# Third head's queries moved between the first two heads' score and turn work, and a weight conversion moved ahead of a square, in a six-layer fp32 kernel

## What is computed

```python
def mla_mixer(xn, cos, sin, w_in, q_norm, w_q_up, kv_norm, w_kv_up, w_out):
    h = xn @ w_in
    q_lat, kv_lat, k_rope, z = jnp.split(h, [...], axis=-1)
    q = (rms_norm(q_lat, q_norm) @ w_q_up).reshape(B, S, N_HEADS, QK_NOPE_DIM + QK_ROPE_DIM)
    q_nope = q[..., :QK_NOPE_DIM]
    q_rope = apply_rope(q[..., QK_NOPE_DIM:], cos[:, :, None, :], sin[:, :, None, :])
    kv = (rms_norm(kv_lat, kv_norm) @ w_kv_up).reshape(B, S, N_HEADS, QK_NOPE_DIM + V_HEAD_DIM)
    k_nope, v = kv[..., :QK_NOPE_DIM], kv[..., QK_NOPE_DIM:]
    k_rope = apply_rope(k_rope, cos, sin)
    o = causal_block_attention(q_nope, q_rope, k_nope, k_rope, v)
    return (o.reshape(B, S, D_INNER) * jax.nn.silu(z)) @ w_out
```

## Time and profile before

| what | us |
|---|---|
| median of 3 runs | 2753.75 |
| lowest and highest of them | 2748.66, 2754.22 |
| the profiled execution | 2755.0 |
| its span, from the first to the last instruction | 2753.2 |

### The profile page before, as it was taken

How to read it: one execution, slowest core, us unless ns; L and a number is a source line. 1 busy time by engine, 2 the same in 40 slices (tenths; PEclk the granted TensorE clock), 3 DMA queues, 4 the chain that set the end, 5 groups by cost and what they waited for, 6 DMA issues and landing times.

```text
span 2753.2 us, 31973 instructions
## 1 busy us (share of the span) xinstructions
PE 2706.2 (98%) x12918; PEld 2265.5 (82%) x12918; DVE 1581.5 (57%) x2307; ACT 1156.2 (42%) x1834; POOL 628.5 (23%) x401
## 2 busy tenths in 40 slices
PE   8999999999999999999999999999999999999998
PEld 6888888888878888888888887878888888778886
DVE  6656555344465646565565787644445678734443
ACT  4323322222356636432235777422224767522223
POOL 1000111011136626300005542410113442411100
PEclk9999999999999999999999999999999999999999
DMA  4332323323222222222322211223233221233332
GB/s 153 100 100 92 103 93 100 100 92 100 91 69 64 65 76 65 91 94 98 100 92 94 77 55 46 84 85 98 94 100 102 70 70 32 77 92 94 98 100 69
DMA packets 69412, 238.78 MB, mean 87 GB/s; under 512 B 7696, under 2 KB 10256, under 8 KB 69264
## 3 DMA queue, kind: packets, MB, share of 16 engines
q1 hardware_dynamic: 69264, 236.73, 26.8%
HBM read 234.60 MB, written 2.10 MB: 86 GB/s over the span
## 4 chain that ended last, share of the span: by engine, by line
PE 93%; DVE 4%; POOL 1%; ACT 1%; issue 1%; DMA 0%; SPq 0%; POOLq 0%; DVEq 0%; ACTq 0%
PE ps L414 29%; PE ps L416 29%; PE ps L415 29%; PE ps L510 1%; POOL acc L2280 1%; PE ps L729 1%; PE ps L728 1%; PE ps L440 1%; DVE xl L1518 1%; POOL t L2465 1%; PE ps L714 0%; DVE x L1540 0%; PE ps L571 0%; PE ps L570 0%; DVE ptl L1514 0%
## 5 line engine op out<-in xcount | busy, mean ns | idle before, releaser
L895 ACT ACTIVATE wh<-raw 128x1024 fp32r<-128x1024 f32 (+2 forms) x453 | 465.1, 1028 | 755.9 <-PE ps L416 750.7
L414 PE MATMUL ps<-xh,wh 128*128 128x512 f32 x1920 | 754.2, 393 | 0.0
L416 PE MATMUL ps<-xh,wl 128*128 128x512 f32 x1920 | 747.5, 389 | 0.0
L415 PE MATMUL ps<-xl,wh 128*128 128x512 f32 x1920 | 747.3, 389 | 0.0
L1506 DVE TENSOR_TENSOR wl<-raw,wh 128x1024 fp32r<-128x1024 f32 (+1 forms) x339 | 447.1, 1319 | 155.3 <-ACT wh L895 155.2
L414 PE MATMUL ps<-yh,wh 128*128 128x512 f32 x1088 | 427.7, 393 | 10.6 <-DVE yl L1514 9.0
L415 PE MATMUL ps<-yl,wh 128*128 128x512 f32 x1088 | 424.9, 391 | 0.0
L416 PE MATMUL ps<-yh,wl 128*128 128x512 f32 x1088 | 424.9, 391 | 0.0
L414 PEld LDWEIGHTS ps<-xh,wh 128*128 128x128 f32 x1920 | 360.6, 188 | 77.1 <-issue 2.6
L415 PEld LDWEIGHTS ps<-xl,wh 128*128 128x128 f32 x1920 | 360.6, 188 | 76.5 <-issue 2.6
L416 PEld LDWEIGHTS ps<-xh,wl 128*128 128x128 f32 x1920 | 360.4, 188 | 74.8
(11 more groups left out here) (255 smaller groups left out, 3667.6 us busy)
## 6 DMA issues: line engine op xcount, KB each, us to landing
raw<-in_ff SPq DMA_DIRECT2D x120, 512.0 KB, 3.6
raw<-in_pool_in SPq DMA_DIRECT2D x64, 512.0 KB, 3.3
raw<-in_conv_in SPq DMA_DIRECT2D x64, 512.0 KB, 3.3
raw<-in_pool_out SPq DMA_DIRECT2D x32, 512.0 KB, 3.3
raw<-in_qk SPq DMA_DIRECT2D x32, 512.0 KB, 3.6
raw<-in_pool_grp SPq DMA_DIRECT2D x16, 512.0 KB, 3.3
raw<-in_conv_out SPq DMA_DIRECT2D x16, 512.0 KB, 3.3
raw<-in_mla_z SPq DMA_DIRECT2D x16, 512.0 KB, 3.6
```

The source lines that it names most:

```text
L414: pe.do.matmul(o, lh, rh_, start=start, stop=False)
L415: pe.do.matmul(o, lh, rl_, start=False, stop=False)
L416: return pe.do.matmul(o, ll, rh_, start=False, stop=stop)
L895: act.do.activation(h[:, 0:ncol], r[:, 0:ncol], ACT.Copy).then_inc(*mark("whi", ("whi", k)))
```

## The change

In the first place, the two query products of head 2 are taken out of their place behind `turn(0)`. `rope_up(2)` goes between `qn 1` and `scores(1)`, and `q_up` of head 2 between `scores(1)` and `turn(0)`. ACT's `swap` of `qr 2` goes ahead of `turned(0)`, and DVE's `turned_cos(2)` ahead of `turn_low(0)`. POOL's program is not edited. In the second place, ACT asks in the turn of each of the first three rows of the last projection for the weights three units ahead, where it asked for two; DVE does so between `add_out` and `x_low`. All later heads and rows keep their order.

```diff
@@ pe_program, mla_layer
                 q_up(("qn", 1), unit["qo", 0], (0, 128, 256))
+                rope_up(2)
                 for h in range(1, 15):
                     scores(h)
+                    if h == 1:
+                        q_up(("qn", 2), unit["qe", 2], (0, 256, 512))
                     turn(h - 1)
                     if h % 2:
-                        rope_up(h + 1)
-                        q_up(("qn", h + 1), unit["qe", h + 1], (0, 256, 512))
+                        if h > 1:
+                            rope_up(h + 1)
+                            q_up(("qn", h + 1), unit["qe", h + 1], (0, 256, 512))
                         k_up(h + 1, unit["ke", h + 1], 0)
@@ act_program, mla_layer
                 for h in range(1, 15):
+                    if h == 1:
+                        swap("m", None, 2, ps("qr", 2), ("mm", "qr", 2))
                     turned(h - 1)
                     if h % 2:
                         taking("qe", h + 1)
                         scores(h)
-                        swap("m", None, h + 1, ps("qr", h + 1), ("mm", "qr", h + 1))
+                        if h > 1:
+                            swap("m", None, h + 1, ps("qr", h + 1), ("mm", "qr", h + 1))
@@ act_program, mla_layer
                 for m in range(3):
-                    taking("mo", 1, m)
+                    weights(unit["mo", 1, m] + 3)
                     done(m)
@@ dve_program, mla_layer
                 for h in range(1, 15):
                     scores(h)
+                    if h == 1:
+                        turned_cos(2)
                     turn_low(PTL, PTH, ("m", h - 1))
                     if h % 2:
                         taking("qe", h + 1)
                         sums(h)
-                        turned_cos(h + 1)
+                        if h > 1:
+                            turned_cos(h + 1)
```

## The result

The changed kernel takes 2743.6 us (median of 6 runs, 2742.2 to 2746.6), the kernel before 2753.9 (6 runs, 2748.7 to 2755.0). One execution in the experiments took 4531 us at a mean granted clock of 0.555 and counts in no range and no ratio here.

The account below looks back on a forecast made before the run. TensorE bounds the kernel, busy 2706 of 2753 us. From the profiled 2755.0, plus 0.45 (first edit), less 1.8 (second), gives 2753.65; with that execution 1.25 above the median, 2752.4 us, range 2748.0 to 2755.0.

Parts of the forecast that it names:

- The bank of `qr 2` that holds it back: Ahead of `qr 2`: its bank is freed by `k_low(1)` only at 819.65, so TensorE still stalls 1.2 us.
- the order of what comes late next: Head 2, behind `kn 2`: `mz 2` is late next, its weights behind `turned(0)` on ACT, then POOL's low part of 2.40 us.
- the swap at no cost: ACT's `swap` of 2.40 us fits behind `silu(0)` in 2.46 us of idle time, so it costs nothing.
- the new stall at `mz 2` and its releaser: Between `kn 2` and `mz 2` TensorE stalls about 2.6 us, released at 833.0 by POOL's low part.
- So 4.0 us of work leave the chain and only 1.35 us are gained: First edit, without clock: `mz 2` starts at 833.0 instead of 834.37; 1.25 us gained after a slow first start.
- the net with the clock: First edit, if the clock falls again at the new stall: 1.25 - 1.72 = -0.45 us, a slight loss.
- Rival 3: First edit works as it reads: all three stalls and the low clock go, 7.3 us, 2746.4 us; chance 0.04.
- The clock term at this place: Behind the new stall at `mz 2` the clock falls again, costing 1.72 us; bounds 0 and 3.4.
- The second edit's local gain: Last projection: row 3's weights come earlier, removing the 1.55 us stall; 1.8 us gained, bounds 1.4 and 1.9.
- It is kept to the end: The last projection's 1.8 us gain lasts to the kernel's end, since later stalls hang only on TensorE's own work.
- Rival 1: The clock stays up in the new stall at `mz 2`: 3.05 us gained in all, 2750.7 us; chance 0.30.

Follow-up runs that it names:

- the first edit alone: The changed kernel with the last projection as before, so only head 2's query products are moved: median 2754.3 us, ratio to before 1.0005.
- the changed kernel again: The changed kernel, unaltered, measured a second time against before: median 2742.7 us, ratio 0.9971.
- the changed with eight more: The changed kernel plus eight 128x512 matmuls, result overwritten, in one projection of the second pooling layer: median 2752.0 us, ratio to before 1.0007.
- the squares' swap: Last head's sum of squares put behind the last stick-breaking head's scores in the last two layers: 2744.8 us in before, 2742.0 in the changed kernel.

## Why the prediction was wrong

**The first edit's steps were right.** The bank of `qr 2` that holds it back (1.2, measured 1.22), the order of what comes late next, the swap at no cost, the new stall at `mz 2` and its releaser: all as worked out, and `mz 2` starts 29.14 us after the value product where before took 30.81, 1.67 earlier for a forecast 1.35. "So 4.0 us of work leave the chain and only 1.35 us are gained" holds, and the net with the clock, forecast at -0.45, is 0.0 with a fall in both kernels and 0.1 without one in either. Rival 3, that it works as it reads, is out. The clock term at this place was sized well too: 1.5 to 1.6 us for a forecast 1.72, and it comes and goes: of the five profiles with the stall of 2.1 us at `mz 2` three have the fall (the first edit alone, the changed kernel again, the changed with eight more), of the four with before's order one has it, before's own. So the prediction took the fall in its baseline for granted from one execution; these are too few to say that the new stall brings the clock down more often.

**The second edit's local gain was right** (1.8; 3.43 for both less 1.67 is 1.76).

**The step that failed** is the last sentence on the second edit: "It is kept to the end, because no stall after it hangs on anything but TensorE's own work." The stalls behind it did stay the same. But the prediction costed the clock only where the edits are, and left the low-clock stretches of the last two layers out of the sum, as if they belonged to those stages. They don't: they depend on where a stall falls in the gate's own time, and the second edit's shift of 1.76 us at 1140 us moved the stall at 1711 to another place in it. That was worth 3.1 us in each of the last two layers, nearly twice the shift each. Of the 12.8 us between the two profiled spans 1.8 are the second edit's, 0.1 the first's, 1.6 the fall at the edited place that one profile has and the other lacks, 7.8 the clock behind the edits (0.57 + 3.10 + 0.67 + 3.07 + 0.43), and 1.5 the draw of the first microseconds. Rival 1 had the idea that a fall may be present or missing, but for the edited place alone. The rows for it were at hand: the trace of before holds six stretches behind 1140 us in which TensorE works at the low clock, and the range should have counted them; two of them were worth 3.1 us each here. The three runs of before that set the width of the range didn't show the group near 2746 either.

**What stays open.** Why the runs of one kernel share the place at all, when the gate keeps its own time, was not tried. It may be argued that each stretch at low clock draws the runs together, since the clock rises again at an instant of the gate's and not of the kernel's. The two profiles of the changed kernel fit: from the first rise of the clock, the first value product is at 787.69 us in one and 786.36 in the other, but behind the fall at `mz 2`, which only the second has, the transposes are at 1611.80 and 1612.01. The spread of 2.5 us with the second edit against 8.7 in before would fit too, but no run isolates it. Nor was it mapped which shifts are good: those tried were 1.8 us both ways, 0.75, and those that the squares' swap brings.

## What to carry to other kernels

When a kernel is bound by TensorE and its trace shows stalls of 1 to 3 us with the clock at 1.2 GHz behind some, an edit anywhere ahead of them can be worth more, or less, than its own stall: before trusting a gain of 0.3%, add a few matmuls whose result is thrown away behind the edit and see whether it stays. The gain that stays is got by covering the stall that brings the clock down; here a swap of two calls gave before 5.6 us and halved the spread of its runs. Look at the single times, too, and not only at the median: those of before come in groups that lie up to 8 us apart, and three runs can miss one. And a stall in which waiting work is placed is not yet won: follow what the moved work's bank waits for, and what it pushes back on the other engines.

## What was unexpected of the hardware

Eight more matmuls made a kernel some 2 us faster by its median, with an interval that just leaves out no change. The Trainium skill, "TensorE: Matmul & The Clock Gate", section "Part 1: The HAM clock gate", has the gate run free of the kernel, so that one kernel's slow matmuls differ from run to run. The traces agree at `mz 2`, where the clock fell in one profile of the changed kernel (825.65 us from the value product to the transposes) and not in the other (824.11), and in the four groups of before; the medians add that the place is not all chance, since the changed kernel with and without eight matmuls differ by 9.3 us, for 1.8 us of work.

The stall of 1.35 us that did most of the harm looks like contention itself. DVE's four operations ahead of it, in before:

```profile
1671.99 1.13 DVE L2034 SCALAR_TENSOR_TENSOR acc<-const,small,acc 128x128 f32<-128x128 f32 x4
...
1708.27 3.28 DVE L2034 SCALAR_TENSOR_TENSOR acc<-const,small,acc 128x128 f32<-128x128 f32 x4
```

and POOL meanwhile:

```profile
1706.08 4.81 POOL L2271 TENSOR_TENSOR wl<-raw,wh 128x1024 fp32r<-128x1024 f32 x2 [11.54 <-ACT wh L895]
```

They took 1.13 us for the head before, when POOL was idle, and 3.28 here. The trace has the single operations: the second of the four starts at 1708.56, 0.11 us behind the start of POOL's second operation (1708.45), lasts 2.47 us where the median one of this line takes 0.35, and ends at 1711.03, 0.15 us behind POOL's end (1710.88). Of the 32 operations of this line one other is as long, in the last layer at 2340.17. The Trainium skill, "SBUF — State Buffer", section "Who interferes with whom", has a DVE instruction with two inputs in SBUF contend with a POOL instruction that reads SBUF, over ports that one of the two holds alone. These rows agree with it. No experiment moved POOL's work away, so this is read from the rows and not shown.
